# Gate blocks of a hybrid layer kernel as pairs of seven quarter products (one Trainium2 core)

## The reference

```python
def short_conv_mixer(b, c, u, conv_w, w_out):
    z = c * u
    z = lax.conv_general_dilated(z, conv_w[:, None, :], ..., padding=[(CONV_WIDTH - 1, 0)],
                                 feature_group_count=D_CONV)     # three causal taps per feature
    return (b * z) @ w_out
...
def hybrid_layer(x, positions, norm_mix, w_in, ...):
    h = rmsnorm(x, norm_mix)
    proj = h @ w_in
    cb, cc, cu, q, k, v, g, ga, gb = jnp.split(proj, split_points, axis=-1)
    y_conv = short_conv_mixer(cb, cc, cu, conv_w, w_conv_out)
    y_ret = retention_mixer(q, k, v, g, positions, ret_norm, w_ret_out)
    merged = jax.nn.sigmoid(ga) * y_conv + jax.nn.sigmoid(gb) * y_ret
    x = x + merged @ w_o
    h2 = rmsnorm(x, norm_mlp)
    return x + jnp.square(jax.nn.relu(h2 @ w_up)) @ w_down
```

## Time and profile before

| | us |
|---|---|
| median of three runs (lowest, highest) | 2440.93 (2440.51, 2441.65) |
| the profiled execution's own time | 2441.64 |
| its span, first to last instruction | 2439.8 |
| TensorE busy | 2426.2 (99%) |
| VectorE busy | 1372.9 (56%) |
| ScalarE busy | 952.8 (39%) |
| POOL busy | 1373.7 (56%) |

### The profile page before, as it was taken

How to read it: one execution, slowest core, us unless ns; L and a number is a source line. 1 busy time by engine, 2 the same in 40 slices (tenths; PEclk the granted TensorE clock), 3 DMA queues, 4 the chain that set the end, 5 groups by cost and what they waited for, 6 DMA issues and landing times.

```text
span 2439.8 us, 34632 instructions
## 1 busy us (share of the span) xinstructions
PE 2426.2 (99%) x12088; PEld 2019.4 (83%) x12088; DVE 1372.9 (56%) x1942; ACT 952.8 (39%) x1363; POOL 1373.7 (56%) x1682
## 2 busy tenths in 40 slices
PE   9999999999999999999999999999999999999999
PEld 7888888888998888888888889988777777888887
DVE  8884412368766768844123666538866665623333
ACT  5331232242543523312322424424577776422222
POOL 5556655556766755566555567657332334555554
PEclk9999999999999999999999999999999999999999
DMA  5222222232433422222222324353211112232322
GB/s 195 82 70 95 96 98 98 95 147 69 173 108 118 173 96 86 70 96 97 98 96 95 146 69 173 110 202 100 71 51 42 61 43 71 91 103 94 102 90 93
DMA packets 64912, 247.79 MB, mean 102 GB/s; under 512 B 7200, under 2 KB 9888, under 8 KB 63520
## 3 DMA queue, kind: packets, MB, share of 16 engines
q1 hardware_dynamic: 62496, 218.13, 26.6%
q10 hardware_dynamic: 2304, 28.17, 2.9%
HBM read 244.17 MB, written 2.10 MB: 101 GB/s over the span
## 4 chain that ended last, share of the span: by engine, by line
PE 92%; DVE 3%; ACT 2%; issue 1%; POOL 1%; DMA 0%; DVEq 0%; SPq 0%; ACTq 0%; POOLq 0%
PE ps L709 87%; PE ps L1092 1%; PE ps L1105 1%; PE ps L1121 1%; PE ps L1060 1%; POOL w_lo L606 1%; ACT prob L1737 0%; DMA w_raw<-weights 0%; ACT set_hi L1424 0%; PE ps L1126 0%; PE ps L784 0%; PE ps L900 0%; DVE sq_q L2554 0%; PE ps L1075 0%; POOL set_lo L627 0%
## 5 line engine op out<-in xcount | busy, mean ns | idle before, releaser
L606 POOL TENSOR_TENSOR w_lo<-w_raw,w_hi 128x256 fp32r<-128x256 f32 x1448 | 1190.5, 855 | 866.7 <-ACT w_hi L1345 645.1
L709 PE MATMUL ps<-H_hi,w_hi 128*128 128x512 f32 x1616 | 641.8, 397 | 0.2 <-DVE H_lo L2505 0.2
L709 PE MATMUL ps<-H_hi,w_lo 128*128 128x512 f32 x1616 | 629.7, 390 | 0.0
L709 PE MATMUL ps<-H_lo,w_hi 128*128 128x512 f32 x1616 | 629.2, 389 | 0.0
L1345 ACT ACTIVATE w_hi<-w_raw 128x1024 fp32r<-128x1024 f32 x295 | 310.1, 1054 | 468.6 <-PE ps L709 468.3
L709 PEld LDWEIGHTS ps<-H_hi,w_hi 128*128 128x128 f32 x1616 | 303.4, 188 | 69.1 <-issue 8.7
L709 PEld LDWEIGHTS ps<-H_lo,w_hi 128*128 128x128 f32 x1616 | 303.6, 188 | 65.2 <-issue 4.5
L709 PEld LDWEIGHTS ps<-H_hi,w_lo 128*128 128x128 f32 x1616 | 303.2, 188 | 63.9
L709 PE MATMUL ps<-A_lo,w_hi 128*128 128x512 f32 x744 | 289.6, 389 | 0.0
L709 PE MATMUL ps<-A_hi,w_hi 128*128 128x512 f32 x688 | 268.6, 390 | 0.0
L709 PE MATMUL ps<-A_hi,w_lo 128*128 128x512 f32 x688 | 267.8, 389 | 0.0
(11 more groups left out here) (331 smaller groups left out, 4035.6 us busy)
## 6 DMA issues: line engine op xcount, KB each, us to landing
w_raw<-weights SPq DMA_DIRECT2D x403, 512.0 KB, 3.3
mod_w<-mod_weights ACTq DMA_DIRECT2D x8, 3072.0 KB, 11.0
toeplitz<-biases SPq DMA_DIRECT2D x14, 128.0 KB, 2.1
out<-X SPq DMA_DIRECT2D x7, 256.0 KB, 2.0
X<-x SPq DMA_DIRECT2D x3, 512.0 KB, 7.5
decay_sb<-decay ACTq DMA_DIRECT2D x1, 1024.0 KB, 6.3
ctx_sb<-context ACTq DMA_DIRECT2D x1, 1024.0 KB, 13.8
X<-x SPq DMA_DIRECT2D x2, 256.0 KB, 3.9
```

Of the source, the lines that this page charges most:

```text
L606: last = nc.gpsimd.tensor_tensor(lo[:, c:c + LOW_COLS], w_raw[:, q, c:c + LOW_COLS], hi[:, c:c + LOW_COLS].bitcast(F32), ALU.subtract)
L709: mm = nc.tensor.matmul(dst, w[l], xs[r], start=start and a == 0, stop=stop and a == 2, skip_group_check=joined)
```

## The change

In both hybrid layers the eight b jobs, eight gate b jobs and eight gate a jobs become pairs of seven quarter products. The order of jobs is now: c and u alternating (16), b then gate b as one run of eight pairs, the retention output (8 plain), gate a as a run of four pairs, the convolution output (8 plain), w_o (8 plain). The combinations T of the first norm's stream are made during the c-u stage (M_hi, M_lo). The convolution of a tile follows its c and u; that of the last tile goes into the first pair of the b run, on VectorE. The products b times convolution are rounded by ScalarE (`bz_high`) and their lower parts made by VectorE (`bz_low`) within the gate a run. In all quarter-product runs, the feed-forward ones too, the sum S3 now stands in SBUF (VectorE waits until the S3 of the pair before is used), and the sum S2 comes ahead of S3's lower part. `kept` and `second_out` move to another place in SBUF; `scaled_halves` waits for `t_diffs` before its first scaling, not after its fourth.

```diff
-PAIR_JOBS = 2 * DT
-CONV_JOBS = 3 * DT
+CU_JOBS = 2 * DT
...
-JOB_CONV = JOB_G + G_JOBS
-JOB_RET = JOB_CONV + CONV_JOBS
-JOB_MIX = JOB_RET + PAIR_JOBS
+JOB_CU = JOB_G + G_JOBS
+JOB_B = JOB_CU + CU_JOBS
+JOB_GB = JOB_B + DT
+JOB_RET = JOB_GB + DT
+JOB_GA = JOB_RET + DT
+JOB_MIX = JOB_GA + DT
 EARLY_G = 2
-JOB_O = JOB_MIX + PAIR_JOBS
+JOB_O = JOB_MIX + DT
 JOB_FF = JOB_O + O_JOBS
 FF_GROUP_JOBS = 2 * DT
 LAYER_JOBS = JOB_FF + FF_GROUPS * FF_GROUP_JOBS
...
+FF_RUNS = {ff_run(L, g): DT // 2 for L, g in FAST}
+MIX_RUNS = {L * LAYER_JOBS + first: pairs for L in range(DEPTH) for first, pairs in ((JOB_B, DT), (JOB_GA, DT // 2))}
+RUNS = {**FF_RUNS, **MIX_RUNS}
+STEP_OF = {n0 + 2 * j: j for n0, pairs in RUNS.items() for j in range(pairs)}
...
+        M_hi = at("M_hi", 80 * KB, [4, HALF_K, HALF_T], F32R)
+        M_lo = at("M_lo", 96 * KB, [4, HALF_K, HALF_T], F32R)
...
+        kept = at("kept", 216 * KB, [2, HALF_T])
+        second_out = at("second_out", 218 * KB, [S])
...
+T_HIGH_STEPS = {6: T3, 7: T1, 8: T2, 10: T4}
+BZ_STEPS = ((0, 1, 2), (3,), (4,), (5, 6, 7))
...
-            if FAST_JOBS[n][2] == 0 or piece == "S1":
+            if STEP_OF[n] == 0 or piece in ("S1", "S3"):
...
+                jobs(n + JOB_CU, CU_JOBS, H_hi, H_lo, tiles + TILE_H)
+                pe.wait_ge(t_ready, 4 * (2 * L + 1))
+                fast_run(n + JOB_B, DT)
+                jobs_behind(n + JOB_RET, C_hi, C_lo, tiles + TILE_OG)
+                fast_run(n + JOB_GA, DT // 2)
+                jobs_behind(n + JOB_MIX, C_hi, A_lo, tiles + TILE_BZ)
+                jobs(n + JOB_O, O_JOBS, A_hi, C_lo, tiles + TILE_MIX)
...
+            def bz_high(m):
+                nc.scalar.activation(C_hi[:, m, :], Alf[:, m, :], ACT.Copy).then_inc(bz_high_ready, 1)
+            def mix_run(n0, pairs, gates_from, tiles, bz):
...
+                for j in range(pairs):
+                    n = n0 + 2 * j
+                    more = j + 1 < pairs
+                    copy_first(n)
+                    if j:
+                        piece_highs("S1", n)
+                    if more:
+                        piece_highs("A11", n + 2)
+                    keep_third(n)
+                    if more:
+                        piece_highs("S3", n + 2)
+                    if j:
+                        piece_highs("A22", n)
+                    if not more:
+                        block_high(n0 + 2 * pairs, n)
+                    if more and bz:
+                        for m in BZ_STEPS[j]:
+                            bz_high(m)
+                    keep_second(n)
+                    if not more and bz:
+                        for m in BZ_STEPS[j]:
+                            bz_high(m)
+                    if j:
+                        gate(n - 2, 1)
+                    if more:
+                        piece_highs("S2", n + 2)
+                        piece_highs("S4", n + 2)
+                    if j:
+                        gate(n - 2, 0)
+                    if more:
+                        piece_highs("A12", n + 2)
+                last = n0 + 2 * pairs - 2
+                block_high(n0 + 2 * pairs + 1)
+                gate(last, 1)
+                gate(last, 0)
+                block_high(n0 + 2 * pairs + 2)
...
+            def scaled_halves(L, which):
+                hi, lo, whole, base = T_SETS[which]
+                gain = lambda k: par[:, base + L * PAR_LAYER + k:base + L * PAR_LAYER + k + 1]
+                act.wait_ge(diff_ready, 2 * L + which + 1)
                 for k in range(HALF_K):
-                    last = nc.scalar.activation(T_lo_f[:, T3, k, :], X[:, k, HALF_T:S], ACT.Copy, scale=gain(k))
+                    last = nc.scalar.activation(whole[:, T3, k, :], X[:, k, HALF_T:S], ACT.Copy, scale=gain(k))
                 last.then_inc(diff_scaled, 1)
-                act.wait_ge(diff_ready, L + 1)
                 for k in range(HALF_K):
-                    last = nc.scalar.activation(T_lo_f[:, T1, k, :], T_lo_f[:, T1, k, :], ACT.Copy, scale=gain(k))
+                    last = nc.scalar.activation(whole[:, T1, k, :], whole[:, T1, k, :], ACT.Copy, scale=gain(k))
                 last.then_inc(diff_scaled, 1)
...
+                for a in range(CU_JOBS):
+                    if a + RING - 1 < CU_JOBS:
+                        ahead_at(n + JOB_CU + a + RING - 1)
+                    else:
+                        first_pieces(n + JOB_B, a + RING - 1 - CU_JOBS)
+                    if a == 1:
+                        scaled_halves(L, 0)
+                    if a == CU_JOBS - RING:
+                        nc.scalar.activation(warm[:, :], ones[:, 0:1], ACT.Sigmoid)
+                    if a in T_HIGH_STEPS:
+                        t_highs(L, 0, T_HIGH_STEPS[a])
+                mix_run(n + JOB_B, DT, DT // 2, Af, False)
...
+                def mix_run(n0, pairs, second, first, beside):
+                    for j in range(pairs):
+                        n = n0 + 2 * j
+                        more = j + 1 < pairs
+                        if j:
+                            add_c22(n - 2)
+                            sum_of("S1", n)
+                        if more:
+                            sum_of("S3", n + 2)
+                        if j:
+                            second_sum(n - 2)
+                            second(n - 2)
+                        if more:
+                            sum_of("S2", n + 2)
+                            sum_low("S3", n + 2)
+                            sum_low("S2", n + 2)
+                            sum_of("S4", n + 2)
+                        if not more:
+                            beside(j, 0)
+                        if j:
+                            first(n - 2)
+                        if more:
+                            sum_low("S4", n + 2)
+                            beside(j, 0)
+                    last = n0 + 2 * pairs - 2
+                    beside(pairs - 1, 1)
+                    fence()
+                    add_c22(last)
+                    beside(pairs - 1, 2)
+                    second_sum(last)
+                    second(last)
+                    first(last)
...
+                def bz_second(m):
+                    V.tensor_tensor(Alf[:, m, :], second_out[:, :], Alf[:, m, :], ALU.mult).then_inc(bank_free, 1)
+                def bz_first(m, src):
+                    V.tensor_tensor(halves(Alf[:, m, :]), src, halves(Alf[:, m, :]), ALU.mult).then_inc(bank_free, 1)
+                def gate_second(dst):
+                    V.tensor_tensor(dst, second_out[:, :], rstd[:, :], ALU.mult).then_inc(bank_free, 1)
...
+                def bz_lows(j, part):
+                    for m in BZ_STEPS[j] if j + 1 < DT // 2 else BZ_STEPS[j][part:part + 1]:
+                        bz_low(m)
...
+                for m in range(DT):
+                    if m == 0:
+                        t_diffs(0)
+                    q, ahead = 2 * m % RING, n + JOB_B
+                    rs = r + (JOB_CU + 2 * m) // RING
+                    job_done(rs, q)
+                    V.tensor_tensor(Af[:, 3, :], ps[:, q, :], rstd_sq[:, :], ALU.mult).then_inc(bank_free, 1)
+                    fence()
+                    if m == 6:
+                        sum_of("S3", ahead)
+                    job_done(rs, q + 1)
+                    V.tensor_tensor(z[:, m % 2, 2:S + 2], Af[:, 3, :], ps[:, q + 1, :], ALU.mult).then_inc(bank_free, 1)
+                    fence()
+                    if m == 6:
+                        sum_of("S2", ahead)
+                        sum_of("S4", ahead)
+                    if m < DT - 1:
+                        convolved(m)
+                    if m in (1, 2, 3):
+                        t_sums(0, (T3, T2, T4)[m - 1])
+                    elif m == 4:
+                        t_lows(0, T3)
+                        t_lows(0, T1)
+                    elif m == 5:
+                        t_lows(0, T2)
+                        t_lows(0, T4)
+                    elif m == 6:
+                        sum_low("S3", ahead)
+                    elif m == 7:
+                        sum_of("S1", ahead)
+                        sum_low("S1", ahead)
...
+                def last_convolved(j, part):
+                    if j == 0:
+                        convolved(DT - 1)
+                mix_run(n + JOB_B, DT, b_and_gate_second, b_and_gate_first, last_convolved)
+                for m in range(DT):
+                    dve.wait_ge(ev_ready, L * EV_LAYER + EV_RET + 2 * (m // 2) + 2)
+                    job_done(r + (JOB_RET + m) // RING, m % RING)
+                    V.tensor_tensor(Af[:, m, :], Af[:, m, :], ps[:, m % RING, :], ALU.mult).then_inc(bank_free, 1)
+                    first_pair(n + JOB_GA, m)
+                mix_run(n + JOB_GA, DT // 2, lambda n: gate_second(Clf[:, 2 * STEP_OF[n] + 1, :]),
+                        lambda n: gate_first(Clf[:, 2 * STEP_OF[n], :], first_bank(n)), bz_lows)
+                for m in range(DT):
```

(72 more changed lines are left out.)

340 lines of the change are left out of this document (147 added, 193 removed).

## The result

The changed kernel takes 2445.74 us (median of 20 runs, 2443.97 to 2447.96); the kernel before, in runs beside it, 2441.78. The ratio is 1.0017, with an interval of 1.0011 to 1.0023. So it is 0.17% slower: a measured loss, though within the 0.2% that the prediction counted as no change. The forecast was 2433.0, with 2427.5 to 2437.5 as its range: the time is 8 us above the upper end. The profiled execution took 2445.65 (span 2443.8).

What follows compares the result with a forecast made beforehand. TensorE, busy 99% of the span, was taken as the bound, VectorE as second bound of a run. 19.2 - 2 x (2.5 + 2.6) = 9.0, less 1, gives 8.0 off 2440.93: 2433 us, range 2427.5 to 2437.5.

Steps and rivals of the forecast that it cites:

- The gain of 19.2: Both hybrid layers: 24 plain blocks (130.56 us) become 12 pairs (120.96 us) per layer, 9.60 us each, 19.2 us saved.
- The c-u stage at nothing: Building the halves of the first norm's stream during the c and u products was costed at no time.
- S3's operands: S3 in SBUF, feed-forward runs: up to 0.4 us more per pair on VectorE against up to 0.67 saved, taken as 0.
- second sums, S2 and products: VectorE operations reading two SBUF tensors beside POOL's work: 1 us taken off the gain, half of their longest durations.
- 0.7 to spare: Steady mixing pair: VectorE's first half ends at 9.4 us, TensorE asks for the bank at 10.08, so no wait.
- The lock: Shared SBUF port pair of VectorE and GpSimd, locked per instruction; said to speak against putting S3 in SBUF.
- The b run's 2.5: First pairs of each b run: waits at C11's copy, S1 of pair 1, A11 of pair 2 and after, 2.5 us.
- The gate-a run's 2.6: First pairs of each gate-a run: S1 of pair 0 0.7, A11 of pair 2 1.5, with the copy 2.6 us.
- The feed-forward runs at nothing: New S2 order and S3 in SBUF there: between 0.5 us lost and 0.5 gained per run, taken as 0.
- Rival (b): VectorE lags 0.3 us in 20 of 24 pairs, taking 6 more; gain 2 to 4, near 2438; chance 0.16.
- Rival (c): Slower: VectorE's cycle of 11.2 us passes 10.88, all 24 pairs lose 0.3; 2449 with first waits; chance 0.06.

## Why the prediction failed, step by step

- **The gain of 19.2** held: seven quarters cost 10.08 us in every kernel here, and the best loses only 0.6 over them in a gate-a run.
- **The c-u stage at nothing** held: the last 21 plain blocks ahead of the first b run, five of gate g and the 16 of c and u, take 114.66 us, as 21 blocks from the same place on do in the kernel before.
- **S3's operands.** This is the step that failed. I had the lock in hand and saw it at work in the earlier trace rows, yet took 1 us off for it in the whole kernel, for "second sums, S2 and products". Second sums have one operand in PSUM (`second_out<-ps,kept`) and stay at 0.41 to 0.43 in all 44 cases, and S3's lower part, which reads two SBUF tiles, wasn't in the term at all. By the two medians above, S2's sum grows by 0.37 and S3's lower part by 0.53 in a steady pair, 0.9 where I had counted 0.7 to spare and had S3's lower part at 0.69; undoing it gives 9.4 us back. The row to take was the long end of the two-tile sums, 1.07, for both operations and not for one, because GpSimd works through just that part of the pair (all 35 of each overlap its pieces); for the lower part, at 1.22, even that is too little.
- **The lock.** S3's lower part takes 1.22 beside GpSimd and 0.69 without, and GpSimd's pieces grow as well. The rule of the Trainium skill (SBUF — State Buffer, section "SBUF: two separate sides") agrees: a VectorE operation with two SBUF inputs and a GpSimd one that reads SBUF share a port pair, which one of them holds for its whole instruction. I named it as speaking against the change, and priced it as if it rarely struck.
- **The b run's 2.5** was nearly right without that, in part by luck: with S3 in PSUM 2.9, with A11 of pair 2 at 1.39 (I had 1.4). The copy cost 0.81 in the first b run, not 0.3 to 0.4, as ScalarE rounds S1 of pair 0 late behind the last tile, and S1 of pair 1 cost 0.50, not 0.2; the 0.5 for pair 3 was only 0.15.
- **The gate-a run's 2.6** was too low: 3.7 with S3 in PSUM. S1 of pair 0 (0.69 against 0.7), the copy (0.48 against 0.4) and A11 of pair 2 (1.68 against 1.5) were as worked out; 0.57 at S1 of pair 1 and 0.27 at A11 of pair 3 I hadn't seen. Two of the three BZ lower parts of pair 0 took 1.24 and 1.22, and I had priced all three at 0.6 to 0.7.
- **The feed-forward runs at nothing.** They lose 5.4 in all instead of 4.35: 0.2 a run, within my half us.
- **Rival (b)**, a lag in every pair by the lock, for which I gave 0.16 and 2438, was the right mechanism, and too cheap. Pairs 3, 5 and 7 paid in the first layer, 3 and 7 in the second, and not every pair; that the late loads choose them is argued from VectorE's waits for blocks and has no run of its own. Rival (c)'s sum was loose: 24 pairs at 0.32 beyond 10.88 are 7.7 us before any first-pair wait.

Of the 12.7 us between forecast and result, S3's place makes 8.4 (9.4, of which I had allowed 1; some 0.7 of it by the clock, see the last section), the gate-a term 2.1 (1.06 in two runs) and the b term 0.8. Another 0.85 is the base: the kernel before took 2440.93 in the runs shown and 2441.78 beside the changed one. The last half us is within what two profiles differ by ahead of the first b run, which starts at 255.32 in the changed kernel and at 255.93 with S3 in PSUM, from the same code.

## What to carry to other kernels

In this kernel an operand moved from PSUM into SBUF made the two VectorE operations that read it beside another SBUF tile 0.4 to 0.5 us longer in 66 of 70 cases, all beside GpSimd's work; the same operation on S4 stayed short where GpSimd stood still. So list every operation that reads the moved tile, look at what GpSimd does at that moment, and price those that meet it at the long end of the nearest two-tile row at least; a median over all of them can hide which ones do. Work put beside a run needs room in the pair it is put into: the same move of the convolution gave nothing with long operations in the pair and 2.5 us without them. When one edit brings a new order and a new place together, measure each alone: here the order was worth 6 us and the place cost 9.

## What else the runs showed

In the second b run of the changed kernel TensorE, at full clock until then, waited 1.85 us at A11 of pair 2, and the granted clock fell. The stretches up to the wait and over its end:

```profile
1111.42:1131.90 20.48, 18.18 (x145) 17.37 (x143) 17.46 (x23) 9.01 (x19) 11.12 (x12) 1.00 0.17 52
1131.90:1136.50 4.60, 4.32 (x23) 4.32 (x24) 1.99 (x4) 2.21 (x5) 2.52 (x4) 0.63 0.68 228
```

TensorE's timeline at the end of the wait:

```profile
1132.18 0.50 PE L723 MATMUL ps<-H_hi,set_hi 128*128 128x256 f32 x1 [1.85 <-DVE A_lo_f L2371]
```

For 17 matmuls the distance from start to start was 0.21 instead of 0.12, which is the lower of the two levels (1.2 GHz) in place of 2.4: 1.5 us. An equal wait in the first b run (1.84 us, to 276.09) had no such fall, so a wait can cost more than its length, but doesn't always. It is no single case: 14 of the 20 runs of the changed kernel have a mean granted clock below 1.00 (0.998 or 0.999), with a median of 2446.2 us against 2445.0 for the other six; where in those runs it fell isn't recorded. All ten runs with S3 in PSUM are at 1.00, so of the 9.4 us between the two kernels about 0.7 comes by the clock, an estimate from these medians.

The convolution's first operation, which reads one tile, took 0.98 us beside GpSimd in pair 0 of both b runs, against the 0.486 of the earlier trace rows and 0.49 in the kernel in which GpSimd has little to do: a single SBUF input isn't safe from this either.
